# The four output-mean products of the first mixer at other places in a head, their logarithms in one run

## The reference, cut to what matters

```python
def gdn_mixer(h, w_in, conv_w, a_log, dt_bias, out_norm, w_out):
    ...
    g = -jnp.exp(a_log...) * jax.nn.softplus(a... + dt_bias...)
    o = gated_delta_rule_chunked(q, k, v, beta, g)      # uses exp of cumulative sums of g (the decays)
    o = rmsnorm(o, out_norm) * jax.nn.silu(z...)        # mean of squares over 128 channels of each head
    return o.reshape(B, L, GDN_V_W).astype(h.dtype) @ w_out
```

## Time and profile before

| | us |
|---|---|
| median of 3 runs | 2247.55 |
| lowest and highest | 2247.19 and 2250.03 |
| profiled execution | 2246.09 |
| its span, first to last instruction | 2244.3 |
| TensorE busy with matmuls in it | 2155.3 (96%) |
| VectorE busy | 970.8 (43%) |
| ScalarE busy | 747.7 (33%) |
| the eight heads, first to last product | about 77 to 741 |

### The profile page before, as it was taken

The page is one execution under the profiler, slowest core; times in us unless marked ns, Lnnn a source line. Parts: engine busy times, 40 slices in busy tenths (PEclk is TensorE's granted clock), DMA queues, the critical chain, the costliest instruction groups (busy, mean ns, idle before and its releaser), DMA issues.

```text
span 2244.3 us, 37249 instructions
## 1 busy us (share of the span) xinstructions
PE 2155.3 (96%) x16267; PEld 1578.6 (70%) x16267; DVE 970.8 (43%) x1885; ACT 747.7 (33%) x1393; POOL 0.2 (0%) x4
## 2 busy tenths in 40 slices
PE   6999999999999988999999997999998999999999
PEld 5787887787788875555555543575575578888888
DVE  2554554554553103233333203563356555466522
ACT  4435435435432112434343214433444430000000
POOL 0000000000000000000000000000000000000000
PEclk9999999999999999999999998999999999999999
DMA  5312222222222321111211212211000215323230
GB/s 177 96 57 82 84 64 86 83 61 85 69 76 77 104 72 42 33 34 34 65 52 38 70 43 61 76 40 49 23 6 0 76 38 146 94 75 94 71 122 19
DMA packets 200603, 150.06 MB, mean 67 GB/s; under 512 B 16360, under 2 KB 198122, under 8 KB 200058
## 3 DMA queue, kind: packets, MB, share of 16 engines
q1 hardware_dynamic: 200442, 147.69, 22.1%
HBM read 143.41 MB, written 4.26 MB: 66 GB/s over the span
## 4 chain that ended last, share of the span: by engine, by line
PE 89%; DVE 6%; ACT 3%; issue 1%; DMA 0%; SPq 0%; ACTq 0%; DVEq 0%
PE PS L2403 14%; PE PS L1616 12%; PE PS L1626 6%; PE PS L713 5%; PE PS L775 5%; PE PS L451 4%; PE PS L1368 4%; PE PS L1377 3%; PE PS L1370 3%; PE PS L719 2%; PE PS L1547 2%; PE PS L836 2%; PE PS L756 2%; PE PS L757 2%; PE PS L2519 1%
## 5 line engine op out<-in xcount | busy, mean ns | idle before, releaser
L2403 PE MATMUL PS<-hn_all,ring 128*128 128x264 f32 x1536 | 399.8, 395 | 1.2 <-issue 1.2
L2403 PEld LDWEIGHTS PS<-hn_all,ring 128*128 128x128 f32 x1536 | 277.8, 191 | 47.5 <-issue 5.3
L713 PE MATMUL PS<-hn_all,ring 128*128 128x512 f32 x256 | 115.0, 592 | 0.0
L775 PE MATMUL PS<-big,ring 128*128 128x512 f32 x256 | 111.2, 592 | 0.0
L451 PE MATMUL PS<-big,ring 128*128 128x264 f32 x416 | 92.7, 386 | 0.0
L1368 PE MATMUL PS<-ring,hn_all 128*128 128x256 f32 x384 | 89.3, 386 | 2.5 <-ACT scr L1824 2.5
L914 ACT ACTIVATE scr<-PS,scr 128x528 f32<-128x528 f32 (+1 forms) x64 | 34.6, 541 | 165.8 <-DVE scr L1001 165.6
L775 PEld LDWEIGHTS PS<-big,ring 128*128 128x128 f32 x256 | 48.2, 190 | 58.3 <-issue 57.7
L451 PEld LDWEIGHTS PS<-big,ring 128*128 128x128 f32 x416 | 79.0, 190 | 13.5
L1616 PE MATMUL PS<-scr 128*128 128x256 f32 x352 | 84.0, 380 | 1.7 <-DVE scr L2144 1.7
L1616 PE MATMUL PS<-hn_all,scr 128*128 128x256 f32 x352 | 83.3, 379 | 0.4 <-DVE hn_all L2152 0.4
(11 more groups left out here) (475 smaller groups left out, 3843.2 us busy)
## 6 DMA issues: line engine op xcount, KB each, us to landing
ring<-in_w_mod SPq DMA_DIRECT2D x24, 1024.0 KB, 5.2
ring<-in_gdn_w_in SPq DMA_DIRECT2D x16, 1024.0 KB, 5.4
ring<-in_w_in SPq DMA_DIRECT2D x12, 1024.0 KB, 5.4
hn_all<-in_w_ffn_in SPq DMA_DIRECT2D x22, 512.0 KB, 5.3
ring<-in_w_ffn_in SPq DMA_DIRECT2D x22, 512.0 KB, 5.2
ring<-in_mla_w_in SPq DMA_DIRECT2D x9, 1024.0 KB, 5.4
ring<-in_gdn_w_in SPq DMA_DIRECT2D x16, 512.0 KB, 5.2
ring<-in_gdn_w_out SPq DMA_DIRECT2D x8, 1024.0 KB, 5.9
```

The costliest lines, as they stand in the source:

```text
L713: ins = mm(o, wz_pair(p)[:, k, j * P:(j + 1) * P], hq[:, k, :], start=(k == 0), stop=(k == KD - 1))
L775: ins = mm(PS[:, MOUT[m % 2], :], wslot(m % 4, P, 16)[:, k, :], oq[:, k, :], start=(k == 0), stop=(k == 15))
L2403: ins = mm(o, wslot(slot_, 256)[:, k, m * P:(m + 1) * P], hn[:, k, b * HALF:(b + 1) * HALF], start=(k == 0), stop=(k == KD - 1))
```

## The change

The list of side items and ScalarE's order are changed together. The product ms1a goes from the end of part (3, 0) to part (2, 1), behind ms0b; the product ms1b goes from the end of part (3, 1) to part (3, 0), ahead of g0a. ScalarE takes ms1a directly behind ms0b, and ms1b behind v1nb and ahead of the exponential of g0a. The numbers of the items and their turns on banks 3, 4 and 5 follow from the list. VectorE's and SyncE's code stays.

```diff
@@ -349,8 +349,8 @@
             return {(1, 0): q("qa", 0, 4) + own("v0na"), (1, 1): q("qa", 4, 8) + own("m0") + own("v0nb"),
-                    (2, 0): q("qb", 0, 4) + out("ms0a") + own("v1na"), (2, 1): q("qb", 4, 8) + out("ms0b") + own("v1nb"),
-                    (3, 0): q("ka", 0, 4) + g("g0a") + own("m1") + out("ms1a"), (3, 1): q("ka", 4, 8) + g("g0b") + out("ms1b"),
+                    (2, 0): q("qb", 0, 4) + out("ms0a") + own("v1na"), (2, 1): q("qb", 4, 8) + out("ms0b") + out("ms1a") + own("v1nb"),
+                    (3, 0): q("ka", 0, 4) + out("ms1b") + g("g0a") + own("m1"), (3, 1): q("ka", 4, 8) + g("g0b"),
                     (4, 0): q("kb", 0, 4) + g("g1a") + own("kna"), (4, 1): q("kb", 4, 8) + g("g1b") + own("knb"),
@@ -2819,16 +2819,15 @@
                     raw("qb", n)
                 else:
                     early_part("w0a", i)
-                means("ms0b")
+                means("ms0b", "ms1a")
                 natural("v1nb", i)
+                means("ms1b")
                 if nxt:
                     decay("g0a", n)
                 mod_row("m1", i)
-                means("ms1a")
                 if nxt:
                     raw("ka", n)
                     decay("g0b", n)
-                means("ms1b")
                 if i > 0:
                     out_rstd(i - 1)
```

## The result

The changed kernel takes 2238.21 us (median of 5 runs, 2236.35 to 2240.32), against 2247.55 us (median of 5) before: a ratio of 0.9958, 95% interval 0.9942 to 0.9973. It is faster by 9.3 us where 3.7 were forecast, and lies outside the range of 2240.0 to 2248.5. Its profiled execution has a span of 2236.7 us, 7.6 less than before.

The account below looks back on a forecast made before the run. TensorE was taken to bound the kernel, with 89% of the chain that ended last. The wait at (5, 1), 2.3 us, plus junctions, 1.4, gave 3.7 us off the median of 2247.55: forecast 2243.9 us, whole range 2240.0 to 2248.5.

Parts of the forecast that it names:

- 24 loads less: ScalarE's table loads in heads 1 to 6: four of six go per head, 30.8 us of ScalarE, none of it time itself.
- wait of line 2549: TensorE's 0.5 us wait at part (5, 1) in heads 2, 3, 4 and 6 goes: 0.58 x 4 heads = 2.3 us.
- Junctions: On TensorE, no full product has to follow m1 any more: 0.2 us a head in heads 1 to 7, 1.4 us.
- Undisturbed pitch: Length of one head without an issue wait: 83.84 us falls to 83.06 in heads 2, 3, 4 and 6.
- Slack at (4, 0): TensorE's part (4, 0) needs VectorE's level 3 subtraction, now later; 0.6 us of slack stays, costed at nothing.
- Both own gains: The wait at (5, 1) gone, 2.3 us, and the cheaper product order around m1, 1.4 us: 3.7 us together.
- what the change makes later: Delays to g0a's exponential, level 3's subtraction, copies, m1 and SyncE's queue; costed at nothing, m2's weights still landing early.
- issue waits: TensorE waits of 1.5 and 1.2 us in heads 1 and 5, put down to nothing the profile shows.
- the issue waits vanish: Rival: one or both waits in heads 1 and 5 do not return, 1.2 to 4.9 us more gained; 2240.5 us, chance 0.17.
- slower: Rival: new issue waits where instructions arrive late, 3.4 us each; two make 2250.7 us; two or more had chance 0.06.
- The drain rule: About 1380 ns of drain added per ScalarE table load; at (4, 0) 1.38 us, giving 2248.6 us; late-load case 1 in 100.

Follow-up runs that it names:

- the second pair: The kernel before and the changed kernel, both profiled again without edit: 2245.21 us (ratio 0.999) and 2237.12 us (ratio 0.9946).

## Why the prediction was right and wrong

**Right, by its steps.** 24 loads less, at the lines named. No wait of line 2549 left, 2.85 us in its place. Junctions 0.20 a head against 0.2. Undisturbed pitch 83.06 us, the number forecast. Slack at (4, 0) of about 0.6, as forecast; the 0.2 us that I took there for the semaphore stood in no row, and the rows have 0.1. From a load's start to the next activation it is 1.29 us, with no drain in it. Both own gains, 1.35 + 2.32 = 3.7 us, came as summed.

**The step that failed** is one sentence under "what the change makes later": the products m1 move 0.9 us later, "and with them the queue of SyncE". I asked whether those weights still land in time. I costed the move at nothing, and did not ask what else uses the DMA engines when they start. The burst that m1's end sets off went behind a fetch of TensorE's own instructions instead of in front of it in head 1 (in head 5 so in one profile, and early enough in the other). The issue waits of both heads went, and that was worth 3.41 + 1.48 us. In head 4 the changed kernel has one of up to 1.48 us that the kernel before has not. Net, the term put at nothing measured 3.4 us in the first pair of profiles. With it the forecast would have been 2247.55 - 7.1 = 2240.5, just inside my range; the median of 2238.21 lies 2.2 us below that, and this rest is open.

**The rival** "the issue waits vanish" named the right place and the right price (3.4 us in head 1, 1.2 to 4.9 in all), but stood at 0.17 with 2240.5 us. Its argument against itself, that TensorE comes to those points with the same number of instructions and only 0.2 us earlier, was true and beside the point. What counts is the order of two events some 0.7 us apart: the start of the burst, which m1's end sets off, and the instruction at which a fetch comes due. The edit takes ms1a and ms1b from behind m1 to ahead of it, so m1's end, and the burst with it, comes later in the stream, and the fetch does not. The first profile showed both waits as "issue", a name for no cause that the profile shows, and I took them for fixed. The rival "slower" had waits at new places right: head 4's is one, and with 192 instructions more the kernel before has four. Its price of 3.4 us for each was too high for most: head 4's cost 1.48 us. Only those of 2.1 and 2.4 us in head 7 of the two kernels with 192 more, with half clock behind them, cost more (82.95 - 78.48 = 4.5 and 82.36 - 77.75 = 4.6 us, each with a small wait).

**The drain rule** that the prediction took from the Trainium skill (ScalarE: Activation LUTs, "What ACT_TABLE_LOAD costs") would have made (4, 0) wait in six heads. No profile of the changed order has such a wait, and in the rows above the logarithm ends at 344.79, the load starts at 344.81 and the exponential at 346.10.

**Open.** The profiles give 7.1 us (584.66 to 577.58) and 7.9 us (the second pair) in the heads, the timed medians 9.3 and 10.1. The interval of the first comparison, 6 to 13 us, holds them; that of the second, 8.3 to 15.7, just does not hold the 7.9. So a gain of 9 to 10 us is measured, and only 7 to 8 of it are explained. Whether unprofiled runs have longer issue waits than profiled ones was not tried. The part behind head 7's part (5, 0) varied from 1550.3 to 1554.5 us between the profiles, without an order that follows the edits, and this was not followed up.

## What to carry to other kernels

Where the trace shows "issue" waits on the engine that bounds a kernel, look at which weight loads run just before them and what sets those loads off; moving a product moves its load's trigger, and the time of the load belongs in the sum even if its data is early. Test it by changing the trigger alone, and time an edit of a few us in a second phase of the instruction stream (some instructions more in front) before calling it worth more than its own terms. Sorting ScalarE's functions by table pays only what the late result cost the bounding engine: here 31 us of loads gave 2.3.

## What the runs showed of the hardware

A burst of 1 MB of weight loads took 3.5 to 5 us, seldom up to 6 (296 GB/s over 180.40 to 184.00 in the kernel before). A 16 KB fetch takes 1.1 us (the middle one of 70). In head 1 of the kernel before, one that came due 0.7 us behind the start of such a burst started only near its end, 2.6 us late. In the same kernel's heads 11 fetches started 2.0 to 2.8 us late inside a burst or at its end, and TensorE stood still behind two. In all 21 issue waits of the thirteen profiles it went on 1.2 to 1.6 us after the fetch had ended (184.78 and 186.14 in head 1 of the kernel before).

After the stops of 1.5 us in head 1 (two profiles of the kernel before), and after those of 2.1 and 2.4 us in head 7 with 192 instructions more, the granted clock was at half for 3.4 us. After the other 17, of 0.2 to 1.4 us, it stayed at full.
